# Second FFN product of a hybrid encoder layer: where the row work stands between the seven-product pairs, and another order in the last pair

## The reference, cut to what matters

```python
gate, up = jnp.split(x @ w_ffn_in, 2, axis=-1)            # w_ffn_in 1024 x 5632
ffn = (jax.nn.silu(gate) * up) @ w_ffn_out                # w_ffn_out 2816 x 1024
return layer_norm(DEEPNORM_ALPHA * x + ffn, ln2_g, ln2_b)
```

## Time and profile before

| | us |
|---|---|
| median of 3 runs | 979.25 |
| lowest and highest run | 978.34 and 1060.41 |
| the profiled execution's own time | 978.15 |
| its span, slowest core (core 4) | 977.1 |
| spans of the 8 cores | 975.5 to 977.1 |

### The profile page before, as it was taken

The page is one execution under the profiler, slowest core; times in us unless marked ns, Lnnn a source line. Parts: engine busy times, 40 slices in busy tenths (PEclk is TensorE's granted clock), DMA queues, the critical chain, the costliest instruction groups (busy, mean ns, idle before and its releaser), DMA issues.

```text
span 977.1 us, 16482 instructions; the slowest of 8 cores (975.5 to 977.1 us)
## 1 busy us (share of the span) xinstructions
PE 932.3 (95%) x5405; PEld 437.2 (45%) x5501; DVE 632.1 (65%) x1050; ACT 436.6 (45%) x719; POOL 256.1 (26%) x280
## 2 busy tenths in 40 slices
PE   4999999999999999999999999999999999999895
PEld 1455544544444444444445444444444444444342
DVE  1323575666766857566668798966575676675776
ACT  1125657575663354444556467654001444442121
POOL 3200000112135334334332355434100233332000
PEclk9999999999999999999999999999999999999998
DMA  8997033474249999622487277775533323221312
GB/s 131 184 172 140 24 86 95 82 129 72 45 72 138 113 149 126 84 66 54 90 254 272 62 173 168 137 184 122 170 129 108 108 88 111 89 81 37 115 44 87
DMA packets 39684, 112.13 MB, mean 115 GB/s; under 512 B 4976, under 2 KB 16888, under 8 KB 38608
## 3 DMA queue, kind: packets, MB, share of 16 engines
q0 software_dynamic: 11104, 41.16, 29.5%
q1 hardware_dynamic: 28496, 69.91, 23.3%
HBM read 132.49 MB, written 30.47 MB: 167 GB/s over the span
## 4 chain that ended last, share of the span: by engine, by line
PE 84%; DVE 5%; issue 4%; DMA 3%; ACT 3%; POOL 1%; DVEq 0%; ACTq 0%; POOLq 0%; SPq 0%
PE ps L233 82%; DMA arena<-xt 2%; DMA arena<-w_bf_cache 1%; ACT arena L597 1%; ACT arena L645 1%; DVE arena L1446 1%; PE ps L1276 1%; DVE arena L1209 1%; POOL arena L147 0%; DVE arena L1509 0%; DVE arena L590 0%; DVE arena L1483 0%; ACT arena L600 0%; PE ps L760 0%; ACT arena L1191 0%
## 5 line engine op out<-in xcount | busy, mean ns | idle before, releaser
L233 PE MATMUL ps<-arena 128*128 128x512 bf16 (+5 forms) x4995 | 914.3, 358 | 34.5 <-DMA arena<-xt 13.9
L233 PEld LDWEIGHTS ps<-arena 128*128 128x128 bf16 (+2 forms) x5091 | 417.0, 98 | 516.3 <-issue 74.4
L1325 ACT COPY arena<-ps 128x512 f32<-128x512 f32 x132 | 76.3, 586 | 132.3 <-PE ps L233 132.2
L1335 POOL TENSOR_TENSOR arena<-arena 128x512 bf16<-128x512 f32 x66 | 89.0, 1349 | 143.2 <-DVE arena L1328 137.5
L1328 DVE TENSOR_TENSOR arena<-arena,ps 128x512 f32<-128x512 f32 x132 | 88.2, 684 | 39.1 <-PE ps L233 38.7
L940 POOL TENSOR_TENSOR arena<-arena 128x512 f32<-128x512 f32 (+1 forms) x48 | 63.9, 1338 | 104.2 <-DVE arena L931 104.2
L1191 ACT ACTIVATE arena<-arena 128x1024 bf16<-128x1024 f32 x26 | 27.5, 1058 | 95.5 <-DVE arena L1620 88.5
L931 DVE SCALAR_TENSOR_TENSOR arena<-arena,ps 128x512 f32<-128x512 f32 x72 | 49.2, 684 | 23.9 <-ACT arena L927 18.0
L1205 POOL TENSOR_TENSOR rs<-mvt,eps_t 128x1 f32<-128x1 f32 x32 | 24.7, 771 | 144.5 <-DVE mvt L1201 91.9
L923 DVE TENSOR_TENSOR arena<-arena,ps 128x512 f32<-128x512 f32 x54 | 37.0, 686 | 35.3 <-ACT arena L920 19.7
L920 ACT COPY arena<-ps 128x512 f32<-128x512 f32 x54 | 31.6, 585 | 55.8 <-PE ps L233 55.8
(11 more groups left out here) (118 smaller groups left out, 573.2 us busy)
## 6 DMA issues: line engine op xcount, KB each, us to landing
arena<-w_bf_cache SPq DMA_DIRECT2D x44, 512.0 KB, 4.5
arena<-u_scratch SPq DMA_DIRECT2D x64, 135.0 KB, 3.4
arena<-x SPq DMA_DIRECT2D x16, 512.0 KB, 13.6
y_scratch<-arena SPq DMA_DIRECT2D x16, 512.0 KB, 6.2
arena<-y_scratch SPq DMA_DIRECT2D x16, 512.0 KB, 5.4
out<-arena SPq DMA_DIRECT2D x15, 512.0 KB, 2.6
arena<-w_f POOLq DMA_DIRECT2D x22, 256.0 KB, 5.0
arena<-w_g POOLq DMA_DIRECT2D x9, 512.0 KB, 20.5
```

Source lines behind the costliest of these rows:

```text
L233: return pe.run(lambda: nc.tensor.matmul(out, lhsT, rhs, start=start, stop=stop, skip_group_check=onto), deps, inc)
L1325: return act.run(lambda: nc.scalar.copy(buf, ps[:, b, :]), deps)
L1335: return pool.run(lambda: nc.gpsimd.tensor_tensor(out=dst, in0=up, in1=gate, op=ALU.mult), deps)
```

## The change

Four things are done.

1. `f2_block(9)` now returns three steps: the small ones (mean, variance, rstd), centre, scale. Before, the small ones were issued at once.
2. The second half of T4, `form_T4(6, 11)`, becomes a fourth step behind these three. All four stand at the head of the list for pair 10, ahead of the sums of pair 12.
3. In the last pair P5 and its read r5 go directly behind P1; P2, P6, P3, P7, P4 follow.
4. Row 14's centre goes ahead of P7's bank read on DVE. Its scale is done by ACT (L1604, activation Identity with a scale per partition) and the addition of b by GpSimd (L1606, tensor_tensor 128x1024 float32). In L1604 and L1606 the arithmetic of L1213 is the same, in two steps.

```diff
+        if last:
+            z, r5 = p5()
+            filler(1)
+        p2()
+        filler(2 if last else 1)
+        r6 = p6()
+        if not last:
+            filler(2)
+            z, r5 = p5()
         filler(3)
...
             stats(tb)
+            center, scale = pair_rows(tb)
+            center()
             p7()
             t = r8 = acc(Xb, L, x, [hb_tok[tb + 1]])
             banks.release(x, t)
-            for f in pair_rows(tb):
-                f()
+            t_row = act.run(lambda: nc.scalar.activation(Xa, Xa, AF.Identity, scale=rs16[:, 16 + tb:17 + tb]),
+                            [pair_tok["y", tb, 0], pair_tok["rs", tb]])
+            t_row = pool.run(lambda: nc.gpsimd.tensor_tensor(out=Xa, in0=Xa, in1=ln2t[1], op=ALU.add), [t_row])
+            dma(sp, out_d[tb * 128:(tb + 1) * 128, :], Xa, s_out[tb % 3], [t_row])
             w, dw = banks.alloc(1)
...
+        if tb == 9:
+            return [small, center, scale]
...
-    form_T4(6, 11, mid_done)
-    rows = [f2_block(9)]
+    rows = f2_block(9) + [lambda: form_T4(6, 11, mid_done)]
```

More of the change, by code:

```diff
@@ L1541, in f2_pair, with p2, p6, p5 @@
         filler(0)
[L1542 to L1554, removed]
+        def p2():
+            y, dy = banks.alloc(1)
+            t = product(y, lambda j: actT[11 + j][:, a], lambda j: w2[11 + j][:, L], True, [dy])
+            t = acc(Xa, L, y, [t, r1], 1.0, sm[tb][0])
+            banks.release(y, t)
+            h[tb] = [t]
+            square(tb, 0, Xa, L, t)
+        def p6():
+            t = product(x, lambda j: S[:, 1, j], lambda j: T2[:, j], False, [r1, forms("T2"), sa["2"]])
+            return acc(Xa, H, x, [t, hb_tok[tb]])
+        def p5():
+            z, dz = banks.alloc(1)
+            t = product(z, lambda j: S[:, 0, j], lambda j: T1j[j], True, [dz, forms("T1"), sa["1a"], sa["1b"]])
+            return z, acc(Xb, H, z, [t, hb_tok[tb + 1]])
+        if last:
[7 more added lines that the diff above has]
+            z, r5 = p5()
         filler(3)
@@ L1614, in pair_rows @@
         return out
+    f2_t = {}
     def f2_block(tb, hooks={}):
@@ L1624, in f2_block, with small, center, scale @@
         t_st2 = ln_stats(xb, [t_h], tb)
[L1625 to L1630, removed]
+        def small():
+            t3 = f2_t["var", tb] = ln_tiny(t_st2, tb, hsum[:, 1, tb:tb + 1], 0)
+            f2_t["rs", tb] = ln_rstd(t3, tb, rs16[:, 16 + tb:17 + tb])
+        def center():
+            f2_t["y", tb] = ln_center(xb, ln2t[0], tb, [f2_t["var", tb], e_state["ln2"]])
+        def scale():
+            t_ln = ln_scale(xb, xb, rs16[:, 16 + tb:17 + tb], ln2t[1], [f2_t["rs", tb], f2_t["y", tb]])
             hb_free[r] = [dma(sp, out_d[tb * 128:(tb + 1) * 128, :], xb, s_out[r], [t_ln])]
@@ L1633, in rows @@
                 load_hb(tb + 3)
-        if tb in (7, 9):
-            return rows
-        rows()
+        if tb == 9:
+            return [small, center, scale]
+        small()
+        if tb == 7:
+            return lambda: (center(), scale())
+        center()
+        scale()
     def y_stores():
```

## The result

| | before | changed |
|---|---|---|
| median | 979.19 us (5 runs) | 972.61 us (5 runs) |
| the profiled execution's own time | 978.15 | 972.61 |
| its slowest span | 977.1 (core 4) | 971.6 (core 7) |
| ratio to the kernel before | | 0.994, 95% interval 0.9926 to 0.9955 |

The ratio is 5.9 us, with an interval of 4.4 to 7.2; 5.0 were forecast. So there is a gain, and it is under the 2% that the prediction names. In later executions beside the experiments the changed kernel had ratios of 0.9940 and 0.9931.

The account below looks back on a forecast made before the run. PE, busy 95% of the span, was taken as the bound. Slowest core after: 976.1 - 2.89 - 1.15 = 972.1, 5.0 us under 977.1; a mean of 978.6 less 5.0 gave 973.5 us, range 971.5 to 977.3.

Parts of the forecast that it names:

- the 2% that the prediction names: Whole kernel: 19.6 us is what a measurement can tell from no change; within 2% was given 0.98.
- Part 1: PE's hole ahead of pair 10's r1 closes with 0.7 us to spare: gain 2.89 us.
- Part 2: Half clock behind the first hole goes: core 4 gains 1.51 us, core 1 nothing, so core 1 ends last.
- Part 3: Last pair: PE 1.9 us ahead, L1533 waits for GpSimd's 2.35 us add, row 15's scale at 22.37: gain 1.15 us.
- (a): Tail: GpSimd's add collides, up to 4.5 us, and the tail loses 1.0 us; time 975.6; chance 0.14.
- (b): Tail: no exclusion bites, GpSimd's rstd behind the add sets it; scale at 22.0, time 973.1; chance 0.07.
- (c): First hole stays in part, r1 missing its 0.7 us: 1 us hole, 1.5 us clock, 976.0; chance 0.09.
- (d): Hole of 2.89 us moves to pair 12, behind P2; slower than before, 979.3; chance 0.03.
- (e): Clock falls anyway on some core, hole or not: 973.5 + 1.0; chance 0.09.
- the sum by way of core 1: Slowest core: core 1 ends last, 976.1 - 2.89 - 1.15 = 972.1, 5.0 us earlier than 977.1.

Follow-up runs that it names:

- e3: Changed kernel, but both halves of T4 stay ahead of block 9's bank read, so only the small steps go behind r1: 973.96 us, ratio 0.9944 to before.
- e4: Changed kernel, but block 9's small steps stay ahead of r1, so only T4's second half moves behind: 975.40 us, ratio 0.9953 to before.
- e2: Changed kernel with block 9 and T4 put back as before, so only the last pair is changed: 979.11 us, ratio 0.9990 to before.
- e9: Changed kernel with T4 cut at 9 in place of 6 and block 9's small steps ahead of r1: 976.83 us, ratio 0.9967 to before.
- e1: Changed kernel with the last pair put back as before, block 9's small steps and T4's second half still moved: 975.03 us, ratio 0.9948 to before.
- e7: Changed kernel without the GpSimd add L1606, so row blocks 14 lack LN2's b: 972.28 us, ratio 0.9918 to before.
- e5: Changed kernel with row 14's centre and scale both on DVE behind r8, as before: 973.85 us, ratio 0.9938 to before.

## Why the prediction was right, and where its sizes were off

**Part 1** held to the hundredths that matter: half of T4 1.75 us, no hole, margins of 0.56 us at r1 (forecast 0.7) and 0.45 at r5 (0.5). The 0.7 was counted from the end of P2's last matmul, and P6 could start 0.16 us before that end. e3 and e4 show that its arithmetic of DVE's order holds step by step.

**Part 2** is the term that was mis-sized. "So core 4 gains 1.51 us too" held, but "core 1 has nothing of this to gain ... so in the new order core 1 ends last" was true of the one execution shown: there the core that reached the first hole last was the one whose clock did not fall. In e2 such a core paid 1.3 us, in e9 the slowest 1.65. Parts 1 and 2 were put at 3.9 us (2.89, and 1.0 from one core being last in place of another); e1 measured 5.1, with 3.8 to 6.4, which just holds 3.9. From e4 to e2 the hole grows by 1.4 us and the ratio by 0.0037, or 3.6 us: some 2.2 us of half clock reach the time at 2.89 us of hole. The half-widths of the two intervals, 1.5 and 1.0 us, add in squares to 1.8, which leaves it between 0.4 and 4.0. The mean of the spans says the same of all cores: from e4 to e2 it grows by 2.6 us (two standard errors 0.6), 1.2 more than the hole. And the slowest core is no exception to it. Over the 33 executions of the kernel before that the ratios use, its mean granted clock was 0.9935, against 0.9950 over all cores; over 14 of the changed kernel it was 0.9961 and 0.9968. A stretch at 0.50 costs half its length, and lowers the mean over a span of 976 us by that half divided by 976. So these differences make an estimate of 2.5 us for the slowest core and 1.8 for all, wherever in the span the clock had fallen. Both errors of size have one sign, this one of about 1 us and that of part 3, 0.4; the measured 5.9, 0.9 above the forecast, has room for both.

**Part 3** was right in kind. L1606 took 2.34 us (forecast 2.35) and L1533 waited to its end, as forecast. The scale came 0.4 us earlier than forecast: P7's read came 1.20 us behind the start of centre 14, where I had put 1.41, so that the add started at 18.41 in place of 18.62; and from the add's end to the scale it was 1.26 us, not 1.40. So the scale gave 1.5 us for 1.15. From scale to end it was 3.71 us in place of 3.84, but on the other cores this stretch was 3.65 to 3.83 before and 3.62 to 3.69 after, so most of that 0.13 belongs to the core.

**Rivals.** (a) falls: no collision stretched the add. (b) had put the scale at 22.0, which is where it came, so that number alone would not have told it from the forecast; it falls by L1533's 1.46 us and by e7. (c) and (d) fall by the timeline, on every core. (e) falls: no stretch of 916 to 950 us was below 1.00 on any core. The rule of the Trainium skill on the shared port pair (SBUF — State Buffer) is borne out: e7 against the changed kernel is the same instruction with and without the GpSimd read beside it, 0.16 and 1.46 us. L1530's 0.21 us beside the add is its other side, an instruction with one tensor input that was not held.

## What to carry to other kernels

Where one engine's bank read gates another, everything ahead of it in its queue adds up, waits on third engines included; the hole is the sum less the slack, and here it could be worked out to a few hundredths from one timeline. Before elementwise work goes to an idle GpSimd, look for an instruction of VectorE on the ending chain that reads two SBUF tensors meanwhile: here even one column of 0.16 us waited for the end of the add, and the move lost 0.3 us. Of a cost that strikes some cores and not others, take it for the slowest too, unless more than one execution shows it spared; and compare the mean of the cores beside the slowest, which scatters less.

## What the runs showed of the hardware that was not expected

In these runs the half clock came with the longer holes, and not sharply. Behind holes of 0.69, 1.49 and 1.76 us no core of the 8 in each profile ran slow; behind 2.29 us five of eight did, and lost 1.6 to 1.7 us each; behind 2.89 us seven of eight before (1.5 to 2.9 us) and six of eight in e2 (1.3 to 1.7 us). In e9 core 1 and core 4 ended equal holes at 918.19 and 918.22 of their spans; core 1 lost 1.7 us and core 4 nothing. What decides between them was not tried.

The exclusion works in both directions. Row 14's rstd on GpSimd took 1.46 us (960.58) beside DVE's centre (960.35, 1.28 us), where it was 0.55 in the pairs before, and 0.55 in e5, where the centre stands behind r8; it was off the path.

The evenness of the kernel before, whose cores ended within 1.6 us of each other in its profile, was chance. In the 33 later executions the spans of its cores lay 2.8 to 7.4 us apart, 5.2 in the median; in 14 of the changed kernel 2.6 to 6.6, 4.9 in the median. In the profiled execution the core that reached the first hole earliest (917.48) lost most to the half clock and the last (920.24) nothing. So the expectation that the changed kernel spreads its cores further, and the sum by way of core 1, both rest on an execution that was not typical.
